# Three 256-column matmuls per weight tile in place of a 512-column and a 256-column one, in the column stages of a two-block transformer kernel

## The reference, cut to what matters

```python
h = modulate(rms_norm(x, g_norm1[l]), sh1, sc1)
qa, ka, va, oa, gates, qb, kb, vb = jnp.split(h @ w_in[l], IN_SPLITS, axis=-1)
...
mixed = jnp.concatenate([h_a, h_b], axis=-1) @ w_out[l]
x = x + ga1[:, None, :] * mixed
h = modulate(rms_norm(x, g_norm2[l]), sh2, sc2)
x = x + ga2[:, None, :] * conv_glu(h, w_up[l], conv_w[l], conv_b[l], w_down[l])
...
u, v, z = jnp.split(h @ w_in, 3, axis=-1)          # second block, first layer
...
cq, ckv, k_rope, z = jnp.split(h @ w_in, [o1, o2, o3], axis=-1)   # second layer
```

## Time and profile before

| | us |
|---|---|
| runs of the kernel | 2397.89, 2404.23, 3952.3 |
| median | 2404.23 |
| the profiled execution's own time | 2397.16 |
| its span, first to last instruction | 2395.3 |
| PE busy | 2353.4 (98%) |
| PEld busy | 2027.0 (85%) |
| DVE busy | 1873.6 (78%) |
| ACT busy | 1116.4 (47%) |
| mean granted TensorE clock | 0.994 |

### The profile page before, as it was taken

How to read it: one execution, slowest core, us unless ns; L and a number is a source line. 1 busy time by engine, 2 the same in 40 slices (tenths; PEclk the granted TensorE clock), 3 DMA queues, 4 the chain that set the end, 5 groups by cost and what they waited for, 6 DMA issues and landing times.

```text
span 2395.3 us, 31737 instructions
## 1 busy us (share of the span) xinstructions
PE 2353.4 (98%) x13036; PEld 2027.0 (85%) x13036; DVE 1873.6 (78%) x2053; ACT 1116.4 (47%) x1383; POOL 0.2 (0%) x4
## 2 busy tenths in 40 slices
PE   5899999999999999999999999999999999999999
PEld 3588888888888888888888888898888888889987
DVE  6889888898888787777878878878787667685754
ACT  2253545545545334555445445644555334555552
POOL 0000000000000000000000000000000000000000
PEclk8899999999999999999999999999999999999999
DMA  9989786695777688777785889766777773764343
GB/s 396 371 327 358 275 293 229 233 332 202 272 266 270 229 299 293 246 246 247 239 276 184 322 321 328 270 231 243 264 263 273 272 281 141 261 223 158 124 160 139
DMA packets 119009, 620.24 MB, mean 259 GB/s; under 512 B 13392, under 2 KB 14672, under 8 KB 76112
## 3 DMA queue, kind: packets, MB, share of 16 engines
q1 hardware_dynamic: 70560, 446.45, 52.2%
q10 hardware_dynamic: 48304, 171.76, 20.0%
HBM read 616.06 MB, written 2.10 MB: 258 GB/s over the span
## 4 chain that ended last, share of the span: by engine, by line
PE 91%; DVE 5%; DMA 3%; ACT 1%; issue 1%; SPq 0%; DVEq 0%; ACTq 0%
PE pm L601 26%; PE ps L601 13%; PE pm L602 13%; PE ps L602 7%; PE pm L640 5%; PE pm L642 5%; PE pm L641 5%; PE ps L642 2%; PE ps L640 2%; PE ps L641 2%; DVE acc_first L1669 2%; DMA e<-in_ada 1%; DVE w_lo L1607 1%; DMA ada<-in_ada 1%; PE px L926 1%; PE px L813 1%
## 5 line engine op out<-in xcount | busy, mean ns | idle before, releaser
L1607 DVE TENSOR_TENSOR w_lo<-raw,w_hi 128x2048 fp32r<-128x2048 f32 (+2 forms) x412 | 892.1, 2166 | 332.7 <-ACT w_hi L1139 331.6
L1139 ACT ACTIVATE w_hi<-raw 128x2048 fp32r<-128x2048 f32 (+2 forms) x412 | 747.1, 1814 | 456.2 <-DMA raw<-in_w_down 126.7
L601 PE MATMUL pm<-h,w_hi 128*128 128x512 f32 x2318 | 800.9, 392 | 0.8 <-DVE ka L1658 0.6
L602 PE MATMUL pm<-h,w_lo 128*128 128x256 f32 x2318 | 641.7, 277 | 0.0
L601 PEld LDWEIGHTS pm<-h,w_hi 128*128 128x128 f32 x2318 | 435.3, 188 | 95.1 <-issue 3.3
L602 PEld LDWEIGHTS pm<-h,w_lo 128*128 128x128 f32 x2318 | 435.2, 188 | 0.2
L601 PE MATMUL ps<-h,w_hi 128*128 128x512 f32 x1186 | 410.7, 391 | 0.8 <-DVE w_lo L1607 0.8
L1619 DVE SCALAR_TENSOR_TENSOR acc<-ada,csil,acc 128x1024 f32<-128x1024 f32 x300 | 383.9, 1280 | 1.5
L602 PE MATMUL ps<-h,w_lo 128*128 128x256 f32 x1186 | 328.2, 277 | 0.0
L601 PEld LDWEIGHTS ps<-h,w_hi 128*128 128x128 f32 x1186 | 222.7, 188 | 48.8 <-issue 2.3
L602 PEld LDWEIGHTS ps<-h,w_lo 128*128 128x128 f32 x1186 | 222.7, 188 | 0.1
(11 more groups left out here) (434 smaller groups left out, 3023.7 us busy)
## 6 DMA issues: line engine op xcount, KB each, us to landing
ada<-in_ada ACTq DMA_DIRECT2D x320, 512.0 KB, 5.6
raw<-in_w_up SPq DMA_DIRECT2D x88, 1024.0 KB, 5.2
raw<-in_w_in SPq DMA_DIRECT2D x56, 1024.0 KB, 6.8
raw<-in_w_down SPq DMA_DIRECT2D x64, 704.0 KB, 5.3
raw<-in_sgu_v SPq DMA_DIRECT2D x32, 1024.0 KB, 5.3
raw<-in_sgu_u SPq DMA_DIRECT2D x32, 1024.0 KB, 5.5
raw<-in_sgu_z SPq DMA_DIRECT2D x32, 1024.0 KB, 4.9
raw<-in_sgu_out SPq DMA_DIRECT2D x32, 1024.0 KB, 5.0
```

The costliest lines, as they stand in the source:

```text
L601: pe.matmul(dst[:, :], wh[:, k, :], hl, start=(kc == 0), stop=False, skip_group_check=True)
L602: mm = pe.matmul(dst[:, 0:T], wl[:, k, :], hi, start=False, stop=last, skip_group_check=True)
L1139: act.activation(hi_(q, n), raw_(q, n), ACT.Copy).then_inc(hi_ready, 1)
L1607: tt_(lo_(q, n), raw_(q, n), whole(hi_(q, n)), ALU.subtract).then_inc(lo_ready, 1)
```

## The change

All three matmuls of a weight tile go to columns 0 to 255 of the bank, as three instructions of 256 columns each. The first two have the same stationary tile. The second half of the bank is no longer written. ACT's copy frees the bank itself, DVE's addition is left out and only its wait remains, and the residual takes one DVE instruction in place of two. Loads, splits, token stages and the order of all else stay.

```diff
@@ columns @@
-                        pe.matmul(dst[:, :], wh[:, k, :], hl, start=(kc == 0), stop=False, skip_group_check=True)
+                        pe.matmul(dst[:, 0:T], wh[:, k, :], hi, start=(kc == 0), stop=False, skip_group_check=True)
+                        pe.matmul(dst[:, 0:T], wh[:, k, :], hl[:, T:2 * T], start=False, stop=False, skip_group_check=True)
                         mm = pe.matmul(dst[:, 0:T], wl[:, k, :], hi, start=False, stop=last, skip_group_check=True)
@@ column_pair @@
-                        pe.matmul(dst[:, :], wh[:, kc, :], hl, start=(kc == 0), stop=False, skip_group_check=True)
+                        pe.matmul(dst[:, 0:T], wh[:, kc, :], hi, start=(kc == 0), stop=False, skip_group_check=True)
+                        pe.matmul(dst[:, 0:T], wh[:, kc, :], hl[:, T:2 * T], start=False, stop=False, skip_group_check=True)
                         mm = pe.matmul(dst[:, 0:T], wl[:, kc, :], hi, start=False, stop=(kc == KC - 1), skip_group_check=True)
@@ column_part @@
-                    pe.matmul(ring[c][:, :], wh[:, kc, :], hl, start=(kc == 0), stop=False, skip_group_check=True)
+                    pe.matmul(ring[c][:, 0:T], wh[:, kc, :], hi, start=(kc == 0), stop=False, skip_group_check=True)
+                    pe.matmul(ring[c][:, 0:T], wh[:, kc, :], hl[:, T:2 * T], start=False, stop=False, skip_group_check=True)
                     mm = pe.matmul(ring[c][:, 0:T], wl[:, kc, :], hi, start=False, stop=(kc == KC - 1), skip_group_check=True)
@@ first_half (ACT) @@
-                act.activation(dst, bank(stage, c)[:, 0:T], ACT.Copy).then_inc(half_out, 1)
+                act.activation(dst, bank(stage, c)[:, 0:T], ACT.Copy).then_inc(freed(stage, c)[0], 1)
@@ second_half (DVE) @@
-                dve.wait_ge(half_out, halved(stage, c))
-                tt_(dst, dst, bank(stage, c)[:, T:2 * T], ALU.add).then_inc(freed(stage, c)[0], 1)
+                dve.wait_ge(*freed(stage, c))
@@ residual (DVE) @@
-                chain.link(stt(xc, src[:, 0:T], mod(gate, c), xc, ALU.mult, ALU.add))
-                stt(xc, src[:, T:2 * T], mod(gate, c), xc, ALU.mult, ALU.add).then_inc(freed(stage, c)[0], 1)
+                stt(xc, src[:, 0:T], mod(gate, c), xc, ALU.mult, ALU.add).then_inc(freed(stage, c)[0], 1)
```

## The result

The changed kernel takes **2444.24 us** (median of 5 runs, 2443.42 to 2445.4); the kernel before took 2402.85 us in the same comparison (5 runs; over all comparisons of this study its runs go from 2394.97 to 2412.78). The ratio is 1.0178, with an interval of [1.0157, 1.02]: slower, by a little less than the 2% that I named as the limit. The profiled execution took 2444.07 us, 46.9 more than that of before, where I had put 75.5. (One of the five runs of before took 3952.3 us; the ratio leaves it out.)

What follows compares the result with a forecast made beforehand. PE's own pace was taken as the bound: 2397.2 + 77 (tiles) + 0.5 (`column_part`) - 2 (DVE relief) = 2472.7 us for a profiled execution, the median put at 2475 us, range 2436 to 2492 us.

Steps and rivals of the forecast that it cites:

- the 2% that I named as the limit: Whole kernel: 2% is 48 us, passed when a tile costs 11.5 ns more, at 353.5 ns per triple.
- DVE's relief: Additions and residual halves removed from DVE, 114 us of work, nearly all beside PE's: taken as 2 us gained.
- the 64 tiles: In `column_pair` DVE sets the pace, 0.794 us per two-tile step; two triples need 0.72 us, so no cost.
- the rival on late instructions: PE's instruction packets: some 29 more, each of 132 holding PE up 0.5 us, adding 66 us: 2539 us; chance 0.04.
- so **360 ns per tile: Column stages: three 256-column matmuls per tile at the head projections' 120.0 ns each, against 342 ns per tile before.
- 4304 x (360 - 342) = 77 us: Main term: 4304 weight tiles in the column stages, each going from 342 to 360 ns, add 77 us.
- wrong if the distances settle at 117 or 113 ns: Sign against the forecast: starts between a tile's matmuls settling there, where it expected 0.12 us between all three.
- the pace of the heads: Head projections in the trace of before: 44 distances between 256-column matmuls, 120.0 ns each, the basis for 360 ns.
- that of the gate projection: Gate projection in the trace of before: 12 matmuls in 1.40 us, 117 ns each, 350 ns per triple.
- The rival that I gave 0.13: Column stages run at the gate projection's pace, 117 to 117.5 ns per matmul: 2430 to 2441 us; chance 0.13.
- the forecast's 0.75: The chance given to the forecast itself, 360 ns per tile.
- the excess over the figures of the Trainium skill: Skill's rule, 2.4 GHz plus 2.5 ns, gives pair 325 and triple 328 ns; the trace has 340 and 360.

Runs made afterwards that it cites:

- the swapped pair: The kernel before with the two matmuls of a tile swapped in the main loop, the 256-column one first: 2395.15 us, ratio 0.9971 to before.

## Why the prediction was right, and where it was off

**Right.** PE's own pace was the bound and stayed it: its waits in the column stages shown were 3.4 us before and are 1.5 us after. The mean of 342 ns per tile before, with a fifth of the tiles slow, holds (342.0, 19%). DVE's relief was put at 2 us and measured at some 1.9, the difference between the changed kernel and that with the additions kept, which is about the size of the spread of either. In `column_pair` a step of two tiles takes 0.79 us after as it did in the earlier trace rows, so the 64 tiles cost nothing. 35 more packets of instructions came, where I estimated 29, and PE's idle time did not grow (span less busy time: 41.9 us before, 39.2 after). No run shows the 0.5 us per packet that the rival on late instructions used.

**Off.** The step that failed is "so **360 ns per tile**": the term 4304 x (360 - 342) = 77 us was 49, and the forecast of 2475 us was 31 us too high. By the prediction's own sign, "wrong if the distances settle at 117 or 113 ns", the pace was forecast wrongly: they settled at 117.8. I took the pace of the heads over that of the gate projection, because the first was longer and without drift. Both are real: the heads keep 120 ns in the trace after as well. But the changed stages run at 117.8, like the gate projection: its 41 distances have a mean of 117.7 in the trace of before (119.3 in that of after), and are as unequal as theirs, 113 to 123 ns, where the first heads have 120 almost without exception. I can't say what makes the two alike: the operand `h` is not it, since the tiles on `glu` and `hx` take 353.3 and 353.4 ns as well. With 353.3 in the sum it comes to 2397.2 + 49 + 0.5 - 2 = 2445 us, 1 us off the profiled 2444.07. The rival that I gave 0.13, settling at 117 to 117.5 ns with 2430 to 2441 us, was the nearest in mechanism and in time; the forecast's 0.75 and the 0.80 for slower by over 2% were too sure, as the ratio came out at 1.0178 and its interval ends at the limit. The measured time lies in the range, 8 us above its lower end, because the range was drawn to take that case in. The mechanism, a third matmul with its load at a price of its own while DVE has slack, was right; that the time fell within the range is owed to the rival's pace and not to the one that I had bet on. I also laid the excess over the figures of the Trainium skill on a larger fixed part; but the two distances of a fast pair, 227 and 113 ns, are as their columns, 2 to 1, which speaks for a higher price per column.

**Where the 13 ns are.** Against the slow pair, 350 ns, the triple costs only 3.3 ns more, a little less than one matmul's surcharge by the rule. Against the fast pair, 340 ns, it costs 13.3, three surcharges where the fast pair has none. The change took the fast pace away from four tiles in five of the first trace, and from 57% of them in the second. That also accounts for a thing that I had passed over, the spread of the runs: the kernel before goes from 2395 to 2413 us, which the share of slow tiles accounts for in its two traced executions, and the changed one, which has one mean pace, from 2443.42 to 2445.4. So "before" is not one number. Against the trace I started from, the change costs 47 us; against the median of 17 runs in a later comparison, 2404.41 us, it costs 40.

**Open.** Why the head projections run at 120 ns, what the 5 ns are and why the token stages' 512-column matmuls are without them, what selects 340 or 350 ns, and why the swapped pair is slow less often.

## What to carry to other kernels

Where PE is the bound, count the matmuls with their loads and not only their columns. A wide moving operand (two products for one load) was worth 11 ns in 342 here, and the vector work saved by giving it up was worth 2 us in 2400, because the vector engine had slack. When two rows of a trace disagree on the price of a form, by 2 ns in 120, and the sum multiplies them by thousands, don't bet on the longer one alone. Here neither its length nor its lack of drift made the heads' row the right one, and the shorter row was. Take the mean where nothing decides, and let the range hold both. And look at the starts in two traces of the same kernel before reading a difference of half a per cent.

## What the runs showed of the hardware that I had not expected

The same stream of matmuls has two stable paces, 340 and 350 ns per pair, which last for hundreds of microseconds and differ between executions of one program. The stream of triples has one mean pace, 353.3 ns, made of unequal distances of 112 to 124 ns. A weight load half as wide frees no time beside 256 streamed columns (353.3 ns per tile both ways), and halves the distance beside 64 (112 to 58.6 ns). In the two kernels with 64 streamed columns per matmul the granted clock was at its lower level, 1.2 GHz, from 950 to 1100 us, while PE was busy by the profile for 150.00 us of 150.
